# A hybrid decoder layer on eight cores: the meta tokens' projection moved into the first block, and a norm stage reordered with one operation on another engine

## Chip, cores and metric

The kernel runs on the 8 cores of one Trainium2 chip. Each core computes one batch element by itself, with the same program and the same weights, so there is no traffic between cores. The metric is the device time of the slowest core, in microseconds (us).

## The reference, cut to what matters

Per batch element: 2048 tokens of width 2048, with 16 learned meta tokens in front, and one layer.

```
u = rms_norm(h)                                   # h = [meta ; x]
z_pool | v_conv | g_conv | gate_a | gate_b = u @ w_in      # 1024|1024|1024|2048|2048 columns
y_a = causal_multiscale_pool(z_pool) @ w_pool_out          # windows 2,4,8,16
y_b = silu(layer_norm(causal_conv31(v_conv * sigmoid(g_conv)))) @ w_conv_out
m   = sigmoid(gate_a) * y_a + sigmoid(gate_b) * y_b
h   = h + rms_norm(m @ w_o)
h   = h + rms_norm(relu(rms_norm(h) @ w_up)**2 @ w_down)   # 8192 hidden
return h[:, 16:]                                  # the meta tokens are dropped
```

The meta tokens reach the output only through the causal windows: the pooling looks back 15 tokens and the convolution 30. So of the meta tokens the kernel needs only z_pool, v_conv and g_conv (3072 of the 7168 columns of `w_in`).

## The kernel before, in words

**Order of the work.** All work is added to a scheduler (`Sched`) in program order; each engine runs its own operations strictly in that order, and the scheduler puts in semaphore waits from the reads and writes of tiles. SBUF tiles lie at fixed offsets, and many of them overlap (dependencies go by 512-byte grains). DMAs of weights are issued from POOL, DMAs of x, the gain rows and the output from SP.

**Weights.** `load_w` (L291) reads 1024 rows by 512 columns of an f32 weight (2 MB in HBM) and writes it as bf16 (1 MB) into the next of the four slots of `ring`. A slot can be loaded again when its last reader on PE is done. One core makes 444 such loads, 124 of them of `w_in`.

**Meta stage (L393 to L407).** The 16 meta tokens are loaded into `xin[0]`, normalised and transposed into `uTm` (L331 to L344, L300, L305). Then for each of 6 column groups (`cg`) of `w_in`, `proj_fm` loads two ring slots and runs 64 matmuls of 16 columns (L380). The results become `halo_z` (groups 0 and 1), the first 16 columns of `c_all[j]` (groups 2 and 3, L298 and L303), and `halo_a` (groups 4 and 5: a sigmoid, L388, and a product with `c_all`, L390). In SBUF, `c_all` overlaps `xin[0]` and `xs`.

**Blocks.** The 2048 tokens are worked on in 4 blocks of 512. For block 0, `phase_A_front` (L275, `nt_front` L413 to L416) and `nt_back` (L429, L436) load x in four tiles of 128 tokens, and make the normalised, transposed `uT_all`; for the other blocks this is done inside the down projection of the block before. Then come: 6 column groups of `w_in` for z, v and g (64 matmuls of 512 columns and two loads each, pooling on DVE), with 4 gate projections and the convolution (`conv_pe`, L480: 31 matmuls per channel group with diagonal weights `dg` that DVE builds, L467) in between; four more gate projections; LayerNorm; `w_po` and `w_co`; `w_o` (L627, L637, L641).

**Norm stage (L645 to L661).** After `w_o`, for each of the four token tiles DVE and ACT compute the reciprocal norm (L313 to L322), DVE multiplies (L653) and adds the tile of x (L656), which SP loads into `xin[tt % 2]`. `xin` overlaps `csq`, into which ACT writes squares until the end of the `w_o` stage. After all four tiles, a second loop calls `nt_front` and `nt_back` for each tile: ACT squares (L413), the norm (L318 to L322), DVE scales into `xs` (L416), PE transposes 16 times 128x128 (L429), DVE multiplies by the gain into `uT_all` in two halves (L436). Then follow `w_up` (16 column groups, L380, L669, L671) and `w_down` (L627).

**PSUM.** `nb(n)` hands out the 8 banks in rotation, leaving out those in `bank_reserved`.

Of the kernel before, what the change touches and what calls it, by code (L numbers as in the profile page):

```python
# [5 lines left out]
F32 = mybir.dt.float32  # L6
BF16 = mybir.dt.bfloat16
AF = mybir.ActivationFunctionType
ALU = mybir.AluOpType
# [4 lines left out]
NMETA = 16  # L14
# [5 lines left out]
TB = 512  # L20
# [121 lines left out]
def build_program(nblk=NBLK):  # L142
# [9 lines left out]
    w_in_d = din("w_in", [D, INC])  # L152
# [18 lines left out]
    S = Sched(nc)  # L171
# [12 lines left out]
    def bump(shape, dt, name):  # L184
        nbytes = int(np.prod(shape[1:])) * (2 if dt == BF16 else 4)
        t = sb(ptr[0], shape, dt, name)
        ptr[0] += (nbytes + G - 1) // G * G
        return t
# [11 lines left out]
    halo_z = bump([128, 8, 15], F32, "haloz")  # L200
    halo_a = bump([128, 8, 30], BF16, "haloa")
    uTm = bump([128, 16, 16], BF16, "uTm")
    wgrp = bump([128, 4, 2, 256], BF16, "wgrp")
    NST = 12
    sts = [bump([128, 16], F32, f"st{i}") for i in range(NST)]
# [41 lines left out]
    def nb(n):  # L247
        r = []
        while len(r) < n:
            bk = banks[bank_rr[0] % 8]  # L250
            bank_rr[0] = (bank_rr[0] + 1) % 8
            if bk in bank_reserved:
                continue
            r.append(bk)
        return r
# [4 lines left out]
    with contextlib.ExitStack() as es:  # L260
# [24 lines left out]
        def load_w(src2d, r0, nk, c0, ncols=512):  # L285
            i = ring_rr[0]
            ring_rr[0] = (i + 1) % 4
            slot = ring[i]
            src = src2d[r0:r0 + nk * 128, c0:c0 + ncols].rearrange("(kc p) n -> p kc n", p=128)
            dst = slot.ap()[:, 0:nk, 0:ncols]  # L290
            S.add("pool", lambda e: e.dma_start(out=dst, in_=src), writes=(slot,), dma_sem=ring_sems[i])  # L291
            return slot

        def copy_scaled(dst_tile, dst_ap, src_tile, src_ap, scale_ap=None, eng=None, extra_reads=()):
            eng = eng or ev_engine()
            if eng == "act":
                if scale_ap is None:
                    f = lambda e: e.activation(out=dst_ap, in_=src_ap, func=AF.Copy)  # L298
                else:
                    f = lambda e: e.activation(out=dst_ap, in_=src_ap, func=AF.Copy, scale=scale_ap)  # L300
            else:
                if scale_ap is None:
                    f = lambda e: e.tensor_copy(out=dst_ap, in_=src_ap)  # L303
                else:
                    f = lambda e: e.tensor_scalar(out=dst_ap, in0=src_ap, scalar1=scale_ap, scalar2=None,  # L305
                                                  op0=ALU.mult)
            S.add(eng, f, reads=(src_tile,) + tuple(extra_reads), writes=(dst_tile,))
# [59 lines left out]
        S.add("dve", lambda e: e.memset(ones_f.ap(), 1.0), writes=(ones_f,))  # L367
        S.add("dve", lambda e: e.memset(halo_a.ap(), 0.0), writes=(halo_a,))

        def proj_fm(wsrc, c0, kchunks, rhs_fn, ntok, bks):  # L370
            nkh = kchunks // 8
            for kh in range(nkh):
                slot = load_w(wsrc, kh * 1024, 8, c0)
                for oc in range(4):
                    def mm(e, kh=kh, oc=oc, slot=slot):
                        inst = None
                        for k in range(8):
                            kk = kh * 8 + k
                            rt, ra = rhs_fn(kk)
                            inst = e.matmul(bks[oc].ap()[:, 0:ntok], lhsT=slot.ap()[:, k, oc * 128:(oc + 1) * 128],  # L380
                                            rhs=ra, start=(kk == 0), stop=(kk == kchunks - 1))
                        return inst
                    rd = [slot] + [rhs_fn(kh * 8 + k)[0] for k in range(8)]
                    S.add("pe", mm, reads=rd, writes=(bks[oc],))

        def glu_into(j, bank, ntok, a_tile, a_ap):
            s = sg[j % 2]
            S.add("act", lambda e: e.activation(out=s.ap()[:, 0:ntok], in_=bank.ap()[:, 0:ntok], func=AF.Sigmoid),  # L388
                  reads=(bank,), writes=(s,))
            S.add("dve", lambda e: e.tensor_tensor(out=a_ap, in0=c_all[j].ap()[:, 0:ntok], in1=s.ap()[:, 0:ntok],  # L390
                                                   op=ALU.mult), reads=(c_all[j], s), writes=(a_tile,))
# [1 line left out]
        dma_in("sp", xin[0], xin[0].ap()[0:NMETA, :], meta_d, xin_sems[0])  # L393
        norm_transpose([(xin[0], xin[0].ap()[0:NMETA, :])], NMETA, gpm,
                       lambda kc, ti: (uTm, uTm.ap()[:, kc, :]))
        for cg in range(6):
            bks = nb(4)
            proj_fm(w_in_d, cg * 512, 16, lambda kk: (uTm, uTm.ap()[:, kk, :]), NMETA, bks)
            for oc in range(4):
                j = (cg % 2) * 4 + oc  # L400
                bk = bks[oc]
                if cg < 2:
                    copy_scaled(halo_z, halo_z.ap()[:, j, :], bk, bk.ap()[:, 1:16])
                elif cg < 4:
                    copy_scaled(c_all[j], c_all[j].ap()[:, 0:NMETA], bk, bk.ap()[:, 0:NMETA])
                else:
                    glu_into(j, bk, NMETA, halo_a, halo_a.ap()[:, j, 14:30])  # L407

        def nt_front(src_t, src_ap, tt):
            xsb = xs[tt % 2]  # L410
            st = st_tile()
            ssa = st.ap()[:, 0:1]
            S.add("act", lambda e: e.activation(out=xsb.ap(), in_=src_ap, func=AF.Square, accum_out=ssa),  # L413
                  reads=(src_t,), writes=(xsb, st))
            rt, ra = rstd_from_ss(st, st.ap()[:, 0:1], 1, 1.0 / D, RMS_EPS)
            S.add("dve", lambda e: e.tensor_scalar(out=xsb.ap(), in0=src_ap, scalar1=ra, scalar2=None, op0=ALU.mult),  # L416
                  reads=(src_t, rt), writes=(xsb,))

        def nt_back(tt, gain):
            xsb = xs[tt % 2]  # L420
# [28 lines left out]
        for b in range(nblk):  # L449
# [46 lines left out]

            for cg in range(4):
                bks = nb(4)
                proj_fm(w_in_d, cg * 512, 16, u_rhs, TB, bks)
                for oc in range(4):  # L500
                    j = (cg % 2) * 4 + oc
                    bk = bks[oc]
                    if cg < 2:
                        z = zx[j % 2]
                        za = z.ap()
                        copy_scaled(z, za[:, 15:527], bk, bk.ap())
                        S.add("dve", lambda e, za=za, j=j: e.tensor_copy(out=za[:, 0:15], in_=halo_z.ap()[:, j, :]),
                              reads=(halo_z,), writes=(z,))
                        wlog = j // 2 + 1
                        src_t = z  # L510
                        for s_ in range(wlog):
                            sh = 1 << s_
                            lo = (1 << (s_ + 1)) - 1
                            dst_t = pt[s_ % 2]
                            S.add("dve", lambda e, d=dst_t.ap(), s=src_t.ap(), lo=lo, sh=sh: e.tensor_tensor(
                                out=d[:, lo:527], in0=s[:, lo:527], in1=s[:, lo - sh:527 - sh], op=ALU.add),
                                reads=(src_t,), writes=(dst_t,))
                            src_t = dst_t
                        dd = dsb[j]
                        S.add("dve", lambda e, dd=dd, s=src_t.ap(), za=za, w=float(1 << wlog): e.scalar_tensor_tensor(  # L520
                            out=dd.ap(), in0=s[:, 15:527], scalar=1.0 / w, in1=za[:, 15:527],
                            op0=ALU.mult, op1=ALU.subtract), reads=(src_t, z), writes=(dd,))
                        S.add("dve", lambda e, za=za, j=j: e.tensor_copy(out=halo_z.ap()[:, j, :], in_=za[:, 512:527]),
                              reads=(z,), writes=(halo_z,))
                    else:
                        copy_scaled(c_all[j], c_all[j].ap(), bk, bk.ap(), eng="act")
            gq = [(0, 0), (0, 1), (1, 0), (1, 1)]
            for half in range(2):
                bks = nb(4)
                proj_fm(w_in_d, (4 + half) * 512, 16, u_rhs, TB, bks)  # L530
                j0 = half * 4
                g_front(j0, bks[0])
                g_front(j0 + 1, bks[1])
                gate_proj(*gq[half * 2])
                conv_pe(j0)
                conv_pe(j0 + 1)
                g_front(j0 + 2, bks[2])
                g_front(j0 + 3, bks[3])
                gate_proj(*gq[half * 2 + 1])
                conv_pe(j0 + 2)  # L540
                conv_pe(j0 + 3)
# [106 lines left out]
            for tt in range(4):  # L648
# [6 lines left out]
                      reads=(h, rt, gbuf), writes=(h,))  # L655
                S.add("dve", lambda e, h=h, xi=xi: e.tensor_tensor(out=h.ap(), in0=h.ap(), in1=xi.ap(), op=ALU.add),  # L656
                      reads=(h, xi), writes=(h,))

            for tt in range(4):
                nt_front(hT[tt], hT[tt].ap(), tt)  # L660
                nt_back(tt, gpl)  # L661

            for cg in range(16):
# [79 lines left out]
```

How the kernel before makes its waits and increments, by code:

```python
        def run(q, e):  # L114
            waited = {}
            for op in self.queues[q]:
                need = {}
                for d in op.deps:
                    sem = d.dma_sem if d.dma_sem is not None else esems[d.eng]
                    v = d.sigval
                    if waited.get(sem, 0) < v and need.get(sem, 0) < v:
                        need[sem] = v
                for sem, v in need.items():
                    e.wait_ge(sem, v)
                    waited[sem] = v
                inst = op.fn(e)
                if op.dma_sem is not None:
                    inst.then_inc(op.dma_sem, 16)
                elif op.signals:
                    inst.then_inc(esems[q], 1)
            if q == "sp":
                for sem in final_waits:
                    e.wait_ge(sem, 16 * self.dma_cnt[sem])
```

## Time and profile before

| | us |
|---|---|
| before, median of 2 runs | 4516.17 |
| lowest and highest | 4496.57, 4535.77 |
| the profiled execution, its own time | 4061.35 |
| its span on the slowest core (core 4) | 4059.5 |
| spans of the 8 cores | 3958.0 to 4059.5 |

The profiled execution is shorter than the two timed runs by 455 us. Durations in the profile belong to that execution. Engines: PE is TensorE's matmul, PEld its weight load, DVE VectorE, ACT ScalarE, POOL GpSimd, SP SyncE. "L380" is line 380 of the kernel. A row of the timeline gives start, duration, engine, line, operation, output and input, the number of merged instructions, and in brackets how long the engine sat idle and who ended that.

### The profile page before, as it was taken

How to read it: one execution, taken by the hardware profiler on the slowest of the kernel's cores; microseconds unless marked ns; L12 is line 12 of the kernel's file. 1: busy time of each engine (PE TensorE's matmuls, PEld its weight loads, DVE VectorE, ACT ScalarE, POOL GpSimd, SP SyncE). 2: the span in 40 equal slices, each digit the busy share in tenths (PEclk: the TensorE clock that was granted, in tenths of full speed). 3: DMA queues.
4: the chain of work that ended last, by engine and by line, in shares of the span. 5: the costliest groups of instructions: out<-in, count | busy, mean ns of one | idle time of the engine just before them, and what ended most of it. 6: DMA issues, size and time to landing. Idle time of an engine off the chain costs nothing.

```text
span 4059.5 us, 40152 instructions; the slowest of 8 cores (3958.0 to 4059.5 us)
## 1 busy us (share of the span) xinstructions
PE 3418.7 (84%) x15920; PEld 1550.7 (38%) x15920; DVE 1029.8 (25%) x1350; ACT 551.7 (14%) x1010; POOL 389.3 (10%) x449
## 2 busy tenths in 40 slices
PE   1799848889999895888999985878999998488997
PEld 1344323334444342334444432333444443233443
DVE  0331541111053234112042243211104315411002
ACT  0112111110011211111001111111001121111000
POOL 1000101001110010110110010000111001011110
PEclk9999979999999997999999997899999999799998
DMA  9976979999996697999998589899999769699996
GB/s 150 160 104 88 130 134 120 117 141 136 152 181 89 93 141 132 123 129 144 151 178 123 82 127 166 92 119 123 147 153 178 112 88 130 113 119 120 137 153 125
DMA packets 472231, 527.76 MB, mean 130 GB/s; under 512 B 8928, under 2 KB 464864, under 8 KB 464864
## 3 DMA queue, kind: packets, MB, share of 16 engines
q0 software_dynamic: 462800, 466.12, 86.9%
q1 hardware_dynamic: 9248, 59.08, 4.3%
q8 instruction: 129, 2.11, 0.2%
q14 instruction: 54, 0.44, 0.0%
HBM read 974.48 MB, written 16.78 MB: 244 GB/s over the span
## 4 chain that ended last, share of the span: by engine, by line
PE 70%; DMA 22%; DVE 5%; issue 2%; ACT 1%; DVEq 0%; POOL 0%; ACTq 0%; POOLq 0%; SPq 0%
PE pb L380 35%; PE pb L627 27%; DMA ring<-w_up 15%; PE pb L480 5%; DMA ring<-w_in 4%; DMA xin<-x 3%; DVE uTall L436 1%; PE pb L564 1%; PE pb L565 1%; DVE xs L416 1%; PE pb L429 1%; DVE hT L656 1%; DVE hT L653 1%; DVE csq L587 0%; ACT xs L413 0%
## 5 line engine op out<-in xcount | busy, mean ns | idle before, releaser
L380 PE MATMUL pb<-uTall,ring 128*128 128x512 bf16 x7680 | 1730.1, 388 | 209.7 <-DMA ring<-w_up 170.0
L380 PEld LDWEIGHTS pb<-uTall,ring 128*128 128x128 bf16 x7680 | 760.6, 100 | 1177.0 <-issue 323.0
L627 PE MATMUL pb<-ring,hid 128*128 128x512 bf16 x4096 | 890.9, 381 | 9.8 <-DVE fT L637 9.8
L627 PEld LDWEIGHTS pb<-ring,hid 128*128 128x128 bf16 x4096 | 402.0, 98 | 497.4 <-issue 18.2
L671 DVE TENSOR_TENSOR hid<-rs 128x512 bf16<-128x512 f32 x256 | 177.2, 692 | 936.4 <-ACT rs L669 936.4
L669 ACT ACTIVATE rs<-pb 128x512 f32<-128x512 f32 x256 | 152.8, 597 | 979.0 <-PE pb L380 975.6
L429 PE MATMUL pb<-identb,xs 128*128 128x128 bf16 x512 | 54.3, 293 | 251.9 <-DVE xs L416 251.9
L291 POOL DMA_DIRECT2D ring<-w_up x128 | 111.9, 874 | 1190.7 <-PE pb L380 1062.8
L627 PE MATMUL pb<-ring,mT 128*128 128x512 bf16 x1024 | 221.7, 379 | 0.0
L637 DVE COPY fT<-pb 128x512 f32<-128x512 f32 x64 | 43.4, 689 | 685.7 <-PE pb L627 648.1
L480 PE MATMUL pb<-ax,dg 128*128 128x512 bf16 x992 | 217.2, 379 | 0.0
L291 POOL DMA_DIRECT2D ring<-w_in x124 | 108.4, 875 | 1109.3 <-PE pb L380 994.9
L291 POOL DMA_DIRECT2D ring<-w_dn x128 | 111.9, 874 | 868.3 <-PE pb L627 707.5
L380 PE MATMUL pb<-pB,ring 128*128 128x512 bf16 x512 | 120.7, 397 | 53.0 <-ACT pB L592 53.0
L429 PEld LDWEIGHTS pb<-identb,xs 128*128 128x128 bf16 x512 | 47.9, 135 | 259.2 <-issue 258.5
L627 PEld LDWEIGHTS pb<-ring,mT 128*128 128x128 bf16 x1024 | 100.2, 98 | 120.8
L480 PEld LDWEIGHTS pb<-ax,dg 128*128 128x128 bf16 x992 | 96.2, 97 | 118.3
L467 DVE TENSOR_TENSOR dg<-identb,wdw 128x3968 bf16<-128x3968 bf16 x32 | 137.0, 4283 | 0.0
L641 ACT ACTIVATE rs<-fT 128x512 f32<-128x512 f32 x64 | 40.1, 627 | 706.5 <-DVE fT L637 702.5
L390 DVE TENSOR_TENSOR ax<-call,sg 128x512 bf16<-128x512 f32 x32 | 22.0, 688 | 375.6 <-ACT sg L388 375.6
L380 PE MATMUL pb<-pA,ring 128*128 128x512 bf16 x512 | 113.1, 379 | 0.0
L380 PEld LDWEIGHTS pb<-pB,ring 128*128 128x128 bf16 x512 | 51.7, 102 | 120.0 <-issue 65.0
(87 smaller groups left out, 1287.4 us busy)
## 6 DMA issues: line engine op xcount, KB each, us to landing
ring<-w_up POOLq DMA_DIRECT2D x128, 1024.0 KB, 25.3
ring<-w_dn POOLq DMA_DIRECT2D x128, 1024.0 KB, 10.8
ring<-w_in POOLq DMA_DIRECT2D x124, 1024.0 KB, 11.6
xin<-x SPq DMA_DIRECT2D x32, 1024.0 KB, 9.8
ring<-w_o POOLq DMA_DIRECT2D x32, 1024.0 KB, 10.7
ring<-w_po POOLq DMA_DIRECT2D x16, 1024.0 KB, 10.8
ring<-w_co POOLq DMA_DIRECT2D x16, 1024.0 KB, 10.8
out<-fT SPq DMA_DIRECT2D x16, 1024.0 KB, 9.6
```

Of the source, the lines that this page charges most:

```text
L291: S.add("pool", lambda e: e.dma_start(out=dst, in_=src), writes=(slot,), dma_sem=ring_sems[i])
L380: inst = e.matmul(bks[oc].ap()[:, 0:ntok], lhsT=slot.ap()[:, k, oc * 128:(oc + 1) * 128], rhs=ra, start=(kk == 0), stop=(kk == kchunks - 1))
L416: S.add("dve", lambda e: e.tensor_scalar(out=xsb.ap(), in0=src_ap, scalar1=ra, scalar2=None, op0=ALU.mult), reads=(src_t, rt), writes=(xsb,))
L429: inst = e.transpose(out=bview[:, i * 128:(i + 1) * 128], in_=xsb.ap()[:, kc * 128:(kc + 1) * 128], identity=ident_b.ap())
L436: S.add("dve", lambda e, o_ap=o_ap, i0=i0, i1=i1: e.tensor_tensor(out=o_ap, in0=i0, in1=i1, op=ALU.mult), reads=(bk, gain), writes=tuple(u ...
L467: S.add("dve", lambda e, d=d, j=j: e.tensor_tensor(out=d.ap(), in0=ident_b.ap().unsqueeze(1).broadcast_to([128, KCONV, 128]), in1=wdw.ap() ...
L480: inst = e.matmul(bk.ap(), lhsT=d.ap()[:, k, :], rhs=a.ap()[:, k:k + 512], start=(k == 0), stop=(k == KCONV - 1))
L564: e.matmul(b_sum.ap(), lhsT=ones_f.ap(), rhs=c_all[j].ap(), start=(j == 0), stop=(j == 7))
L627: inst = e.matmul(bks[tt].ap(), lhsT=act_tiles[kk].ap()[:, tt * 128:(tt + 1) * 128], rhs=slot.ap()[:, k, :], start=(kk == 0), stop=(kk == ...
L637: S.add("dve", lambda e, tt=tt, og=og, bks=bks: e.tensor_copy(out=dst[tt].ap()[:, og * 512:(og + 1) * 512], in_=bks[tt].ap()), reads=(bks[ ...
L669: S.add("act", lambda e, r=r, oc=oc, bks=bks: e.activation(out=r.ap(), in_=bks[oc].ap(), func=AF.Relu), reads=(bks[oc],), writes=(r,))
L671: S.add("dve", lambda e, r=r, jj=jj: e.tensor_tensor(out=hid[jj].ap(), in0=r.ap(), in1=r.ap(), op=ALU.mult), reads=(r,), writes=(hid[jj],))
```

## The change

Two things are changed.

First, the meta stage's projection is gone as a stage of its own. The norm and the transposes of the meta tokens stay where they are. In block 0, `proj_fm` takes one more argument: with `meta_bank` it adds 64 matmuls of 16 columns (`mmeta`) behind the group's own 64, from the same two ring slots, into one more PSUM bank `mbk`. The halos are filled from `mbk`; v goes to a new tile `vm` and not to `c_all`. For the two groups of g the banks are reserved until their sigmoid.

Second, the two loops of the norm stage become one: `nt_front` and `nt_back` of a tile follow directly on its add, and the scale into `xs` is an ACT activation there and no longer a DVE operation.

```diff
+    vm = bump([128, 8, NMETA], F32, "vm")
...
-        def proj_fm(wsrc, c0, kchunks, rhs_fn, ntok, bks):
+        def proj_fm(wsrc, c0, kchunks, rhs_fn, ntok, bks, meta_bank=None):
             nkh = kchunks // 8
+            slots = []
             for kh in range(nkh):
                 slot = load_w(wsrc, kh * 1024, 8, c0)
+                slots.append(slot)
...
+            if meta_bank is not None:
+                def mmeta(e):
+                    inst = None
+                    for oc in range(4):
+                        for kk in range(kchunks):
+                            inst = e.matmul(meta_bank.ap()[:, oc * NMETA:(oc + 1) * NMETA],
+                                            lhsT=slots[kk // 8].ap()[:, kk % 8, oc * 128:(oc + 1) * 128],
+                                            rhs=uTm.ap()[:, kk, :], start=(kk == 0), stop=(kk == kchunks - 1))
+                    return inst
+                S.add("pe", mmeta, reads=slots + [uTm], writes=(meta_bank,))
...
-        for cg in range(6):
-            bks = nb(4)
-            proj_fm(w_in_d, cg * 512, 16, lambda kk: (uTm, uTm.ap()[:, kk, :]), NMETA, bks)
-            for oc in range(4):
-                j = (cg % 2) * 4 + oc
-                bk = bks[oc]
-                if cg < 2:
-                    copy_scaled(halo_z, halo_z.ap()[:, j, :], bk, bk.ap()[:, 1:16])
-                elif cg < 4:
-                    copy_scaled(c_all[j], c_all[j].ap()[:, 0:NMETA], bk, bk.ap()[:, 0:NMETA])
-                else:
-                    glu_into(j, bk, NMETA, halo_a, halo_a.ap()[:, j, 14:30])
...
             for cg in range(4):
                 bks = nb(4)
-                proj_fm(w_in_d, cg * 512, 16, u_rhs, TB, bks)
+                mbk = nb(1)[0] if b == 0 else None
+                proj_fm(w_in_d, cg * 512, 16, u_rhs, TB, bks, meta_bank=mbk)
...
+                    if b == 0:
+                        if cg < 2:
+                            copy_scaled(halo_z, halo_z.ap()[:, j, :], mbk, mbk.ap()[:, oc * NMETA + 1:(oc + 1) * NMETA])
+                        else:
+                            copy_scaled(vm, vm.ap()[:, j, :], mbk, mbk.ap()[:, oc * NMETA:(oc + 1) * NMETA])
...
+                if b == 0:
+                    for oc in range(4):
+                        j = j0 + oc
+                        sm = sg[j % 2]
+                        S.add("act", lambda e, sm=sm, oc=oc, mbk=mbk: e.activation(
+                            out=sm.ap()[:, 0:NMETA], in_=mbk.ap()[:, oc * NMETA:(oc + 1) * NMETA], func=AF.Sigmoid),
+                            reads=(mbk,), writes=(sm,))
+                        S.add("dve", lambda e, sm=sm, j=j: e.tensor_tensor(
+                            out=halo_a.ap()[:, j, 14:30], in0=vm.ap()[:, j, :], in1=sm.ap()[:, 0:NMETA], op=ALU.mult),
+                            reads=(vm, sm), writes=(halo_a,))
+                bank_reserved.update(bks)
                 g_front(j0, bks[0])
+                bank_reserved.discard(bks[0])
...
-        def nt_front(src_t, src_ap, tt):
+        def nt_front(src_t, src_ap, tt, scale_eng="dve"):
...
+            if scale_eng == "act":
+                S.add("act", lambda e: e.activation(out=xsb.ap(), in_=src_ap, func=AF.Copy, scale=ra),
+                      reads=(src_t, rt), writes=(xsb,))
...
                 S.add("dve", lambda e, h=h, xi=xi: e.tensor_tensor(out=h.ap(), in0=h.ap(), in1=xi.ap(), op=ALU.add),
                       reads=(h, xi), writes=(h,))
-
-            for tt in range(4):
-                nt_front(hT[tt], hT[tt].ap(), tt)
+                nt_front(h, h.ap(), tt, scale_eng="act")
                 nt_back(tt, gpl)
```

## Rows read from the trace of the kernel before

**Rows 1.** The profile's page: busy time by engine, and TensorE's clock by slice.

```profile
PE 3418.7 (84%) x15920; PEld 1550.7 (38%) x15920; DVE 1029.8 (25%) x1350; ACT 551.7 (14%) x1010; POOL 389.3 (10%) x449
...
PEclk9999979999999997999999997899999999799998
```

**Rows 2.** The profile's page: the chain that ended last, by line.

```profile
PE pb L380 35%; PE pb L627 27%; DMA ring<-w_up 15%; PE pb L480 5%; DMA ring<-w_in 4%; DMA xin<-x 3%; DVE uTall L436 1%; PE pb L564 1%; PE pb L565 1%; DVE xs L416 1%; PE pb L429 1%; DVE hT L656 1%; DVE hT L653 1%; DVE csq L587 0%; ACT xs L413 0%
```

**Rows 3.** Timeline of core 4, from 0 to 260 us: the meta stage and the first x tiles.

```profile
20.01 1.27 DVE L334 TENSOR_SCALAR xs<-xin,st 16x2048 bf16<-16x2048 f32 x1
...
27.59 1.86 PE L380 MATMUL pb<-uTm,ring 128*128 128x16 bf16 x64 [5.59 <-DVE uTm L305]
...
94.59 1.00 PE L380 MATMUL pb<-uTm,ring 128*128 128x16 bf16 x32 [5.86 <-DMA ring<-w_in]
...
96.73 18.52 SPq L275 DMA_DIRECT2D xin<-x  x4
106.53 1.91 ACT L413 ACTIVATE xs<-xin 128x2048 bf16<-128x2048 f32 x1 [10.29 <-DMA xin<-x]
...
122.10 1.91 ACT L413 ACTIVATE xs<-xin 128x2048 bf16<-128x2048 f32 x1 [8.92 <-DMA xin<-x]
...
125.03 1.29 DVE L416 TENSOR_SCALAR xs<-xin,st 128x2048 bf16<-128x2048 f32 x1
...
133.88 85.89 PE L380 MATMUL pb<-uTall,ring 128*128 128x512 bf16 x384 [1.39 <-DVE uTall L436]
```

**Rows 4.** What the SP queue waited for: total us, times, longest.

```profile
SPq L124 <- DVE haloa L390: 28.3, 1, 28.3
```

**Rows 5.** Ring tile, 134 to 330 us: issue to landing of the 20 loads there.

```profile
DMA to landing us min/median/max: 8.1/10.7/11.6
```

**Rows 6.** Timeline of core 4, 178 to 300 us: block 0 between gate and convolution.

```profile
234.71 13.97 PE L380 MATMUL pb<-uTall,ring 128*128 128x512 bf16 x64 [1.52 <-ACT sg L388]
```

**Rows 7.** Timeline of core 4, 520 to 605 us: the norm stage of block 0.

```profile
549.68 2.29 DVE L656 TENSOR_TENSOR hT<-hT,xin 128x2048 f32<-128x2048 f32 x1 [11.85 <-DMA xin<-x]
551.89 0.15 DVE L313 TENSOR_REDUCE st<-st 128x1 f32<-128x4 f32 x1
...
552.97 2.35 DVE L653 SCALAR_TENSOR_TENSOR hT<-hT,st,gbuf 128x2048 f32<-128x2048 f32 x1
555.49 2.29 DVE L656 TENSOR_TENSOR hT<-hT,xin 128x2048 f32<-128x2048 f32 x1 [0.17 <-DVE hT L653]
...
570.13 1.29 DVE L416 TENSOR_SCALAR xs<-hT,st 128x2048 bf16<-128x2048 f32 x1
...
571.56 1.86 PE L429 MATMUL pb<-identb,xs 128*128 128x128 bf16 x16 [39.86 <-DVE xs L416]
572.68 2.36 DVE L436 TENSOR_TENSOR uTall<-pb,gpl 128x1024 bf16<-128x1024 bf16 x2 [1.26 <-PE pb L429]
574.95 0.14 DVE L318 TENSOR_SCALAR st<-st 128x1 f32<-128x1 f32 x1
...
589.59 2.36 DVE L436 TENSOR_TENSOR uTall<-pb,gpl 128x1024 bf16<-128x1024 bf16 x2 [1.27 <-PE pb L429]
590.96 14.21 PE L380 MATMUL pb<-uTall,ring 128*128 128x512 bf16 x59 [0.63 <-DVE uTall L436]
```

**Rows 8.** Timeline of core 4, 2486 to 2556 us: the norm stage of block 2, fourth tile.

```profile
2524.45 2.29 DVE L656 TENSOR_TENSOR hT<-hT,xin 128x2048 f32<-128x2048 f32 x1 [3.49 <-DMA xin<-x]
```

**Rows 9.** Groups by line and shape, ACT: busy us, mean ns.

```profile
L413 ACT ACTIVATE xs<-hT 128x2048 bf16<-128x2048 f32 x16 | 30.4, 1897 | 0.0
...
L298 ACT ACTIVATE call<-pb 128x512 f32<-128x512 f32 x32 | 19.1, 597 | 90.4 <-PE pb L380 90.4
...
L300 ACT ACTIVATE pA<-pb,psc 128x512 bf16<-128x512 f32 x16 | 10.9, 686 | 1.9 <-PE pb L550 1.4
```

**Rows 10.** Ring tile, 592 to 875 us (up projection of block 0): issue to landing.

```profile
DMA to landing us min/median/max: 11.5/26.9/33.1
```

More of the change, by code:

```diff
@@ L415, in nt_front @@
             rt, ra = rstd_from_ss(st, st.ap()[:, 0:1], 1, 1.0 / D, RMS_EPS)
-            S.add("dve", lambda e: e.tensor_scalar(out=xsb.ap(), in0=src_ap, scalar1=ra, scalar2=None, op0=ALU.mult),
-                  reads=(src_t, rt), writes=(xsb,))
+            if scale_eng == "act":
+                S.add("act", lambda e: e.activation(out=xsb.ap(), in_=src_ap, func=AF.Copy, scale=ra),
+                      reads=(src_t, rt), writes=(xsb,))
+            else:
+                S.add("dve", lambda e: e.tensor_scalar(out=xsb.ap(), in0=src_ap, scalar1=ra, scalar2=None, op0=ALU.mult),
+                      reads=(src_t, rt), writes=(xsb,))
         def nt_back(tt, gain):
@@ L502, in build_program @@
                     bk = bks[oc]
+                    if b == 0:
+                        if cg < 2:
+                            copy_scaled(halo_z, halo_z.ap()[:, j, :], mbk, mbk.ap()[:, oc * NMETA + 1:(oc + 1) * NMETA])
+                        else:
+                            copy_scaled(vm, vm.ap()[:, j, :], mbk, mbk.ap()[:, oc * NMETA:(oc + 1) * NMETA])
                     if cg < 2:
@@ L529, in build_program @@
                 bks = nb(4)
-                proj_fm(w_in_d, (4 + half) * 512, 16, u_rhs, TB, bks)
+                mbk = nb(1)[0] if b == 0 else None
+                proj_fm(w_in_d, (4 + half) * 512, 16, u_rhs, TB, bks, meta_bank=mbk)
                 j0 = half * 4
+                if b == 0:
[9 more added lines that the diff above has]
+                bank_reserved.update(bks)
                 g_front(j0, bks[0])
+                bank_reserved.discard(bks[0])
                 g_front(j0 + 1, bks[1])
+                bank_reserved.discard(bks[1])
                 gate_proj(*gq[half * 2])
@@ L537, in build_program @@
                 g_front(j0 + 2, bks[2])
+                bank_reserved.discard(bks[2])
                 g_front(j0 + 3, bks[3])
+                bank_reserved.discard(bks[3])
                 gate_proj(*gq[half * 2 + 1])
```

## The prediction

> **What bounds the kernel now.** I read the page first. TensorE is busy 84% of the span at a clock near full, no other engine over 25% [rows 1]; the chain that ended last is TensorE for 70%, then waits for `w_up` loads (15%), `w_in` loads (4%) and x tiles (3%) [rows 2]. So the kernel is TensorE with holes in it, and the change works on two kinds of hole: the start, and the norm stage of each block. The timeline of the start shows the first: the 12 weight loads of the meta stage pass at (94.59 - 27.59) / 10 = 6.7 us each, while the 32 matmuls on each take 1.00 us. SP then sits until 96.73 before it can load x, and the first 512-column matmul runs at 133.88 [rows 3]. What it waited for last is the halo's product on DVE, which reads `c_all`, on top of which x is to be loaded [rows 4]. The timeline of the norm stage shows the second: from the first add of x at 549.68 to the first `w_up` matmul at 590.96, 41.28 us, DVE and ACT work through four tiles and TensorE does only transposes [rows 7].
>
> **Part 1, the start.** Twelve loads and 384 small matmuls leave the start, 384 come back in block 0. `vm` takes the place of `c_all`, so the load of x into `xin[0]` waits only for the meta norm, whose last read ends at 20.01 + 1.27 = 21.3 [rows 3]; SP's issue is at about 21.4 in place of 96.73. From that issue to the first block matmul it was 133.88 - 96.73 = 37.15, which contains the landing of two x tiles beside four weight loads still under way, the wait for the next two, and the norms. In the new kernel three to four weight loads are under way at 21.4, so I take the same 37.15: first matmul at 58.6, a gain of 75.3 us. Bounds: if x were to land only behind three weight loads (3 x 6.7 = 20 us, in place of beside them), everything is some 19 us later and the gain is 56; if x lands with less company than before, the 10.3 and 8.9 us that ACT waited for it [rows 3] could lose a third, and the gain is 82.
>
> **Part 2, the meta matmuls in block 0.** They are now on TensorE's own path, behind each of six groups. 64 of them take 1.86 us in one run and 2.00 in two runs of 32 [rows 3]: 6 x 2.0 = +12.0. Block 0 has TensorE working 13.97 us per 64 matmuls, 6.98 per load [rows 6], and loads land 8.1 to 11.6 us after issue [rows 5], so nothing but TensorE sets the pace there and nothing hides the 12 us. Low bound 0 (if the loads set the pace instead), high bound the spacing of the transposes, 1.86 / 16 = 0.116 us each [rows 7], 45 us.
> The Trainium skill's page "TensorE: Matmul & The Clock Gate", section "LDWEIGHTS (loading the stationary operand)", puts a weight load at its columns divided by 1.2 per ns, 107 ns for 128 columns whatever follows; a 16-column matmul can't cover that. By it the 384 pairs would cost 41 us, 29 more than my term. The trace disagrees: 64 pairs passed in 1.86 us, 29 ns each.
>
> Two edges of this part. The two slots of a group are now both held until the meta matmuls behind it, so POOL, whose next load waits for the slot's last reader, issues in pairs every 15.97 us and no longer one per 6.98. Behind it in POOL's queue stand only further weight loads. The first of a pair is needed 15.97 us later, the second 22.9 us later; with a landing of at most 11.6, and one more load's 6.7 for the second (18.3), both are in time, at no cost. And the rotation of the banks shifts in block 0: the gate projection behind the first convolutions no longer needs a bank that waits for a sigmoid, which gives back its 1.52 us [rows 6]: -1.5, with 0 and -3 as bounds. Four small sigmoids and products stand before the first g half's work on DVE; DVE then has the 14 us of a gate projection as cover for two `dg` builds, as before. On SP the four x loads pass nothing else of weight.
>
> **Part 3, the norm stage.** DVE runs strictly in program order. Before, its adds for all four tiles stood ahead of the norms, and ACT's work on one tile ran beside DVE's on the next. Now DVE carries for each tile: norm, multiply, add, then it waits for ACT's square, computes the norm, waits for ACT's scale, for PE's transposes, and does the two gain products; only then comes the next tile's multiply. Queued behind these waits are all later DVE operations of the stage, and TensorE waits for the last of them. The period of a tile, from the reduce to the next reduce: reduce to multiply 552.97 - 551.89 = 1.08; multiply to add 2.52; the add 2.29 [rows 7]; hand-over 0.15; square to the scale's start 125.03 - 122.10 = 2.93 [rows 3]; the scale on ACT 1.90 + 0.09 = 1.99 (the 2048-wide activation, plus what a scale operand added to the 512-wide one, 686 - 597 ns) [rows 9]; hand-over 0.14; transposes to first product 572.68 - 571.56 = 1.12; both products 574.95 - 572.68 = 2.27 [rows 7]. Sum 14.49.
> From the first add to the first `w_up` matmul: 4 x 14.49, less the first tile's 1.08 and 2.52 (they lie ahead of that add), less the last pair's 2.27 and plus 590.96 - 589.59 = 1.37 (the matmuls start after the first of the two): 53.5 against 41.3, +12.2 us. In block 2 the fourth tile's add waited 3.49 for x [rows 8]; that wait is hidden now, so +8.5 there. Four blocks: 3 x 12.2 + 8.5 = +45.1. The scale's move alone is 0.70 of the period. Bounds: if the tiles overlapped in spite of the order, the stage would be DVE's work alone, about 37 us, -17 in all; if hand-overs are each worse, +60. Does anything hide it? All four ring slots are full in the stage, so no loading is gained, and TensorE's clock is at its lower level (1.2 GHz) there before and after.
>
> **Sum.** -75.3 + 12.0 - 1.5 + 45.1 = -19.7 us. The gain at the start is nearly all given back. The profiled execution is 4061.35, so 4041.7, a factor of 0.9951. The timed runs lie 455 us above it, which no row explains; I carry the factor over: 4516.17 x 0.9951 = 4494.
>
> **The rivals.**
> 1. The loads set the pace. The loads of `w_in` passed at 6.7 us and TensorE takes 6.98 per load: a margin of 4%. The timed runs are 455 us longer; if all that sat in the 444 loads it would be 1.02 us each, and block 0 would be bound by loads. Then the 12 loads taken away are worth 12 us more and the meta matmuls cost nothing: -44, 4472. Against it: the landings of 8 to 12 us in block 0 [rows 5].
> 2. The norm stage overlaps after all (ACT takes work off DVE, a tile's norm runs beside the next one's add): -17 in place of +45.1, -81.7 in all, factor 0.980, 4425. For it: DVE is the busiest in the stage; against it: DVE's strict order, in which every term above is a chain.
> 3. Slower: the held slots starve TensorE in block 0. If the first load of a pair took the 26.9 us that `w_up` loads take from issue to landing under pressure [rows 10], and not 10.7, each group would wait 26.9 - 15.97 = 10.9, six groups 66: +46 in all, factor 1.0113, 4567. It decides as soon as the wait is over 19.7 / 6 = 3.3 us a group. Against it: [rows 5].
> 4. Each meta matmul carries its whole weight load (PEld's own time per load, were it not overlapped): the price is inside the bounds of part 2, up to +45 in place of +12.0, so +13 in all, 4531. Against it: the 29 ns of [rows 3].
>
> **How the numbers follow.** My forecast 0.60; the loads set the pace 0.20; overlap 0.05; starved groups 0.12; full weight loads 0.03. The range has to hold 8 in 10: the forecast, rival 1 and rival 4 with the spread of the two runs shown (20 us each way) and the bounds of the start (56 to 82) reach from about 4440 to 4550; overlap and the worst of the starved case stay out: 4435 to 4550. A measurement of this kernel can tell about 2% from no change, that is 4426 and 4606. Faster by over 2%: half of the overlap and a small part of rival 1, and what I have not thought of: 0.08. Slower by over 2%: the starved case beyond its price, 0.05. Within 2%: 0.87.
>
> **What would show it.** In the new timeline: x issued by SP near 21 us and the first 512-column matmul near 59; behind each of the first six groups 64 matmuls of 16 columns in about 2 us; POOL's loads of block 0 in pairs, with no wait of TensorE for `w_in` worth naming there; in the norm stage, four adds of x some 14.5 us apart (5.8 before), DVE idle for ACT's scale, and 53 us from the first add to the first `w_up` matmul. I am wrong if the adds stand under 10 us apart, if the first block matmul comes after 70, if TensorE waits over 3 us for a load in each group of block 0, or if the up projection, which no part of the change touches, comes out longer or shorter by tens of us.

## The result, and the profile after

| | us |
|---|---|
| changed kernel, median of 39 runs | 4063.98 |
| kernel before, median of 37 runs | 4132.47 |
| ratio | 0.992, 95% interval 0.9898 to 0.9943 |
| the changed kernel's profiled execution, its time and span | 4035.21, 4033.7 |

Both medians include executions in which the cores of one die show a lower granted clock than the other's (one of the kernel before: 4490.94 us, about 0.80 on one die and 0.94 on the other); the ratio, here and below, compares only the undisturbed ones.

So the change makes the kernel 0.8% faster, some 32 us in 4060 (23 to 41), which is inside the 2% that the prediction called "no change". The time itself, 4063.98, lies far below the stated range of 4435 to 4550.

The start, in the timeline of the changed kernel's slowest core (core 5), answers to [rows 3]:

```profile
24.31 19.24 SPq L276 DMA_DIRECT2D xin<-x  x4
...
34.85 1.91 ACT L413 ACTIVATE xs<-xin 128x2048 bf16<-128x2048 f32 x1 [7.13 <-DMA xin<-x]
...
61.52 15.72 PE L383 MATMUL pb<-uTall,ring 128*128 128x512 bf16 x64 [1.42 <-DVE uTall L440]
...
94.12 13.97 PE L383 MATMUL pb<-uTall,ring 128*128 128x512 bf16 x64
...
94.81 1.75 POOL L292 DMA_DIRECT2D ring<-w_in  x2 [13.67 <-PE pb L393]
...
107.93 1.76 PE L393 MATMUL pb<-uTm,ring 128*128 128x16 bf16 x64
...
109.55 13.97 PE L383 MATMUL pb<-uTall,ring 128*128 128x512 bf16 x64
110.24 1.75 POOL L292 DMA_DIRECT2D ring<-w_in  x2 [13.69 <-PE pb L393]
```

SP issues x at 24.3 and the first 512-column matmul comes at 61.5. Two groups start 109.55 - 94.12 = 15.43 us apart, with the 64 meta matmuls between them, and POOL issues its loads in pairs. What TensorE waited for from 61 to 465 us (total us, times, longest), and the landing of the loads from 61 to 160 us (for [rows 5]):

```profile
PE pb L383 <- ACT pB L618: 13.2, 1, 13.2
PE pb L383 <- DVE uTall L440: 1.4, 1, 1.4
PE pb L590 <- ACT csq L586: 1.1, 1, 1.1
```

```profile
DMA to landing us min/median/max: 9.3/15.3/16.2
```

No load is waited for in block 0, and the sigmoid's wait of [rows 6] is gone. The norm stage of block 0, same core, answers to [rows 7]:

```profile
481.20 2.29 DVE L682 TENSOR_TENSOR hT<-hT,xin 128x2048 f32<-128x2048 f32 x1 [10.93 <-DMA xin<-x]
483.58 1.91 ACT L413 ACTIVATE xs<-hT 128x2048 bf16<-128x2048 f32 x1 [16.12 <-DVE hT L682]
...
486.56 2.00 ACT L417 ACTIVATE xs<-hT,st 128x2048 bf16<-128x2048 f32 x1 [0.41 <-DVE st L323]
488.81 1.87 PE L433 MATMUL pb<-identb,xs 128*128 128x128 bf16 x16 [24.67 <-ACT xs L417]
489.93 2.36 DVE L440 TENSOR_TENSOR uTall<-pb,gpl 128x1024 bf16<-128x1024 bf16 x2 [3.52 <-PE pb L433]
492.20 0.14 DVE L314 TENSOR_REDUCE st<-st 128x1 f32<-128x4 f32 x1
...
495.81 2.29 DVE L682 TENSOR_TENSOR hT<-hT,xin 128x2048 f32<-128x2048 f32 x1 [0.17 <-DVE hT L679]
...
535.20 10.10 PE L383 MATMUL pb<-uTall,ring 128*128 128x512 bf16 x44 [0.62 <-DVE uTall L440]
```

The adds stand 14.61 us apart (5.81 before), and the chain from one to the next is the one that the prediction wrote out: add, square, scale, transposes, products, and only then the next tile's norm. DVE sits idle for 3.52 us before the products.

Each core's trace was cut by the starts of instructions into stages: start (to the first 512-column matmul), block 0's matmuls up to the last of `w_o`, the same of blocks 1 to 3, the four waits from there to the first add of x, the four norm stages (first add to first `w_up` matmul), the four up projections (to the first `w_down` matmul), the four down projections. Means over the eight cores, in us; for the up projections also the least and the most of a core:

```
kernel             start  block0  1 to 3  to add  norm   up (a core's sum)    down
before             135.6  396.6   1216.2   63.5   170.1  1074 (1016 to 1111)  967
changed             60.4  402.7   1218.2   66.9   216.9  1082 (1062 to 1097)  968
e1 fold only        58.8  403.0   1215.3   63.4   168.3  1057 (1042 to 1071)  967
e2 norm only       133.3  397.0   1215.8   65.1   217.0  1061 (1031 to 1076)  968
e3 meta twice       59.1  412.6   1214.0   61.6   216.9  1029 (1014 to 1042)  968
e4 pipelined, ACT   59.0  402.7   1229.1   67.0   122.4  1048 (1025 to 1067)  967
e5 one loop, DVE    59.2  402.6   1228.9   61.5   203.6  1043 ( 994 to 1066)  971
e6 two loops, ACT   59.4  402.3   1221.5   60.4   182.9  1041 (1014 to 1066)  973
e7 pipelined, DVE   59.4  402.9   1215.1   68.1   116.6  1061 (1047 to 1071)  974
e8 up from w_in     59.3  402.9   1215.9   36.1   216.8   889 ( 888 to  890)  964
e9 other pitch      59.0  422.5   1221.4   34.2   216.9   898 ( 889 to  917)  976
e10 tiled w_up      59.2  402.4   1215.1   65.8   112.6   891 ( 888 to  892)  965
```

(In e4 to e6 one pair of cores or another lost some 28 us within a block to a lower clock; that is in "1 to 3". In e9 four cores lost time in this way, two of them some 80 us in block 0.) Two things are to be seen here. The touched stages moved as forecast: start -75.2, block 0 +6.1, norm stages +46.8, together -22.3 (the forecast's terms: -75.3, +10.5, +45.1). And the up projections, which the change does not touch, differ by up to 54 us in their means from one profiled execution to the next, with the same `w_up` loads, and by up to 95 from core to core within one: more than the change is worth.

### The profile page after: what moved, and what is told of

Its sections match the earlier page's. It is cut to its first block, busy times and chain, and to the rows that moved or that the text cites. A ratio compares the mean times of both kernels' runs of the same rounds, so it can differ in the third digit from the quotient of the medians.

```text
span 4033.7 us, 40131 instructions; the slowest of 8 cores (3991.3 to 4033.7 us)
## 1 busy us (share of the span) xinstructions
PE 3407.6 (84%) x15920; PEld 1547.4 (38%) x15920; DVE 1012.7 (25%) x1334; ACT 579.9 (14%) x1024; POOL 378.8 (9%) x437
## 4 chain that ended last, share of the span: by engine, by line
PE 70%; DMA 20%; DVE 5%; ACT 3%; issue 2%; SPq 0%; DVEq 0%; ACTq 0%; POOLq 0%
PE pb L383 36%; PE pb L653 26%; DMA ring<-w_up 14%; PE pb L484 5%; DMA ring<-w_in 2%; DMA xin<-x 2%; ACT xs L413 1%; DMA ring<-w_dn 1%; DVE uTall L440 1%; DVE hT L682 1%; ACT xs L417 1%; PE pb L590 1%; DVE hT L679 1%; PE pb L591 1%; PE pb L433 1%
## 5 line engine op out<-in xcount | busy, mean ns | idle before, releaser
L292 POOL DMA_DIRECT2D ring<-w_in x112 | 97.9, 875 | 1058.1 <-PE pb L383 787.9
```

## The experiments

**e1, the first part alone.** The changed kernel with the norm stage in its old form:

```diff
-                nt_front(h, h.ap(), tt, scale_eng="act")
-                nt_back(tt, gpl)
+
+            for tt in range(4):
+                nt_front(hT[tt], hT[tt].ap(), tt)
+                nt_back(tt, gpl)
```

> Only the first part of the change: the meta projection is folded into block 0, the norm stage is as before. My theory (the terms are right and stand side by side): the first block matmul at about 60 us in place of 135, block 0 from there to the last w_o matmul some 6 to 9 us longer, the rest unchanged: 66 to 70 us off, ratio 0.983. Rival (loads set the pace and the gain at the start is partly met again later, or multiplied): a ratio under 0.978 or over 0.988.

Measured: ratio 0.9809 (0.9778 to 0.984), some 77 us; start 58.8, block 0 +6.4, the rest as before. The ratio lies between the rival's two bounds; its interval just touches the lower one, 0.978.

**e2, the second part alone.** The kernel before, with `nt_front` of the changed one and

```diff
-
-            for tt in range(4):
-                nt_front(hT[tt], hT[tt].ap(), tt)
-                nt_back(tt, gpl)
+                nt_front(h, h.ap(), tt, scale_eng="act")
+                nt_back(tt, gpl)
```

> Only the second part of the change: one loop in the norm stage with the scale on ACT, meta stage as before. My theory (DVE's strict order makes a chain of it): first add to first w_up matmul 54 us in place of 41 to 45, so +46 us in all, ratio 1.011. Rival (the changed kernel is 32 us faster where the steps of the trace add up to some 22, because this part costs less than it seems, for instance since the up projection behind it gives some back): a ratio of 1.005 or less.

Measured: ratio 1.0105 (1.0075 to 1.0135), +42 us; norm stages 217.0 in place of 170.1. So the second part, by itself, makes the kernel slower; the rival's 1.005 lies outside the interval. The product of both ratios is 0.9912 against 0.992 for both together: the parts stand side by side.

**e3, the meta matmuls twice.**

```diff
                 S.add("pe", mmeta, reads=slots + [uTm], writes=(meta_bank,))
+                S.add("pe", mmeta, reads=slots + [uTm], writes=(meta_bank,))
```

> The changed kernel with every group's 64 meta matmuls issued twice (the result is the same). If their price is what the changed kernel's trace shows between the groups (15.43 - 13.97 = 1.46 us each), block 0 gets 6 x 1.5 = 9 us longer from the first block matmul to the last w_o matmul. If loads set the pace there, it gets no longer. If a meta matmul carried a whole weight load, the second set would add over 30 us.

Measured: block 0 412.6 against 402.7, +9.9 us for 384 more matmuls, 26 ns each. They are on TensorE's path, no load hides them, and none adds the time of a whole weight load to it (a weight load's own record lasts 95 ns). (This execution was all the same shorter than the changed kernel's profiled one, because of its up projections, 1029 against 1082: a single execution says nothing of a few tens of us here.)

**e4, the norm stage interleaved.** After `w_o` the four multiplies come first; then, in this order (each a few lines with the operations of before):

```diff
-                nt_front(h, h.ap(), tt, scale_eng="act")
-                nt_back(tt, gpl)
...
+            add_x(0)
+            square(0)
+            add_x(1)
+            norm_scale(0)
+            square(1)
+            nt_back(0, gpl)
+            norm_scale(1)
+            add_x(2)
+            square(2)
+            nt_back(1, gpl)
+            norm_scale(2)
+            add_x(3)
+            square(3)
+            nt_back(2, gpl)
+            norm_scale(3)
+            nt_back(3, gpl)
```

> The changed kernel with the norm stage written in another order: all four multiplies first (beside the wait for x), then adds and norms interleaved so that DVE always has a tile's add or product to do while ACT squares or scales another; the scale stays on ACT. If it is the order of DVE's queue that costs the 54 us and not the engine of the scale, first add to first w_up matmul falls to 28 to 32 us, under the 41 to 45 of the kernel before: 4 x 24 = 96 us off the changed kernel, ratio to before about 0.970. If ACT is what bounds the stage (16 us of squares and scales) or x lands too late, 35 to 40 us and a ratio of about 0.98.

Measured: 122.4 / 4 = 30.6 us a stage, ratio 0.9737 (0.9689 to 0.9786). Same operations, same engines as in the changed kernel, another order: 23.6 us less a stage. Its timeline (core 1, block 0) shows the third and the fourth add 6.6 us apart, with ACT's scale beside them (the first two stand 2.2 us apart, the second and third 9.4):

```profile
492.01 2.29 DVE L690 TENSOR_TENSOR hT<-hT,xin 128x2048 f32<-128x2048 f32 x1
492.22 2.00 ACT L705 ACTIVATE xs<-hT,st 128x2048 bf16<-128x2048 f32 x1 [0.42 <-DVE st L323]
...
495.66 2.36 DVE L440 TENSOR_TENSOR uTall<-pb,gpl 128x1024 bf16<-128x1024 bf16 x2 [1.36 <-PE pb L433]
...
498.58 2.29 DVE L690 TENSOR_TENSOR hT<-hT,xin 128x2048 f32<-128x2048 f32 x1
...
510.17 20.05 PE L383 MATMUL pb<-uTall,ring 128*128 128x512 bf16 x86 [0.69 <-DVE uTall L440]
```

**e5 and e6, order and engine apart.** e5 is the changed kernel with `scale_eng="dve"` in its one loop; e6 has two loops as in e1, but with `scale_eng="act"`.

> The changed kernel with one loop in the norm stage, but the scale back on DVE. By my sum the engine of the scale is 0.70 us and a hand-over of 0.3 out of a tile's 14.6: first add to first w_up matmul 50 to 52 us in place of 54. If the move to ACT were the dear part, it would fall back to 41 to 45.

> The changed kernel with the norm stage in two loops as before, but the scale on ACT. If the order is what costs, first add to first w_up matmul is 44 to 46 us (the 41.3 of before, plus 4 tiles of about 1 us). If the engine is what costs, it stays at 52 to 54.

Measured on core 5, block 0; e5, then e6, timelines:

```profile
478.08 2.29 DVE L682 TENSOR_TENSOR hT<-hT,xin 128x2048 f32<-128x2048 f32 x1 [9.62 <-DMA xin<-x]
...
528.70 16.59 PE L383 MATMUL pb<-uTall,ring 128*128 128x512 bf16 x70 [0.62 <-DVE uTall L440]
```

```profile
479.35 2.29 DVE L682 TENSOR_TENSOR hT<-hT,xin 128x2048 f32<-128x2048 f32 x1 [10.91 <-DMA xin<-x]
...
496.78 2.29 DVE L682 TENSOR_TENSOR hT<-hT,xin 128x2048 f32<-128x2048 f32 x1 [0.17 <-DVE hT L679]
...
524.30 10.91 PE L383 MATMUL pb<-uTall,ring 128*128 128x512 bf16 x43 [0.69 <-DVE uTall L440]
```

One loop with DVE's scale 50.6, two loops with ACT's 45.0, against 41.3 (neither) and 54.0 (both). So in block 0 the order costs 9.0 to 9.3 us a stage and the engine 3.4 to 3.7; they add. Over all cores and blocks the table gives 8.4 to 8.5 and 3.2 to 3.3.

**e7, interleaved, scale on DVE.** e4 with the scale as a DVE operation.

> The interleaved norm stage with the scale on DVE. There DVE has a tile's add or product waiting for it, so its 1.29 us is added to its own queue but the 0.7 us shorter scale and one hand-over less shorten each tile's chain: 28 to 32 us from first add to first w_up matmul, within 2 us of the form with ACT, ratio to before 0.970 to 0.976. If the move to ACT pays once DVE is the busier engine, 2 us or more longer per block than the form with ACT (29.8 to 31).

Measured: 116.6 / 4 = 29.2 us a stage (30.6 with ACT), ratio 0.9692 (0.9633 to 0.9752). Even where DVE is busy, ACT's longer scale and its hand-over do not pay in the traces; the ratios of the two can't be told apart.

**e8, the up projection with w_in's weights.** What remained was the scatter of the up projections. A load reads 2 KB pieces, one of each row; from a piece to the next (the pitch) it is 32 KB in `w_up`, whose rows have 8192 numbers of 4 bytes, and 28 KB in `w_in`. Left out: the up projection's true weights.

```diff
-                proj_fm(w_up_d, cg * 512, 16, u_rhs, TB, bks)
+                proj_fm(w_in_d, (cg % 14) * 512, 16, u_rhs, TB, bks)
```

> The changed kernel, in which the up projection reads its weights from w_in (row pitch 28 KB, the 16 column groups taken modulo 14) in place of w_up (row pitch 32 KB): the same count and size of loads and the same matmuls, on other numbers. It asks what makes the up projection last 240 to 285 us, and what makes this time scatter from run to run by more than the change is worth. If the loads of w_up are slow because of where they lie, the stage falls to 220 to 230 us on all cores, with little scatter, and 160 us or more come off. If the stage is slow because 8 cores load at once whatever they load, it stays at 260 or more.

Measured: every core 222 us a stage, sums of 888 to 890; the cores' spans are 3780 to 3786 where the changed kernel's were 3991 to 4034. The loads of one such stage (core 2, 510 to 750 us), against [rows 10]:

```profile
DMA to landing us min/median/max: 9.0/9.9/17.6
```

The wait ahead of the first add fell too, from 66.9 to 36.1 in four. SP issues x at 464 us, while the first four loads of the coming up projection, issued from 444 to 465 us, are under way (core 5, block 0): beside loads of `w_up` the x tiles took a median of 16.7 us to land, beside loads of `w_in` 9.3.

**e9, the same buffer at another pitch.** Left out, again: the true weights.

```diff
+    w_up_v = w_up_d.rearrange("a (b c) -> (a b) c", b=4)
...
-                proj_fm(w_up_d, cg * 512, 16, u_rhs, TB, bks)
+                proj_fm(w_up_v[(cg // 4) * 2048:(cg // 4 + 1) * 2048, :], (cg % 4) * 512, 16, u_rhs, TB, bks)
```

> The changed kernel, in which the up projection reads the same buffer w_up as if it were a matrix of 8192 rows of 2048 (pitch 8 KB in place of 32 KB): same buffer, same number, size and piece length (2 KB) of reads, other numbers. If the pitch of 32 KB is what makes w_up's loads slow and the up projection scatter, the stage falls to about 222 us on every core as it did with w_in's 28 KB. If it is the place of the buffer or its size, it stays at 250 to 280.

Measured: on the four cores that kept their clock throughout, 889 to 891 for the four stages and spans of 3780 to 3782; of the 32 stages of all cores 28 took 222 to 223 us. The loads of one stage on core 5:

```profile
DMA to landing us min/median/max: 9.3/10.0/10.5
```

It is not the buffer and not its size: 2 KB pieces with a pitch of 32 KB are slow here, pieces of the same length with 8 or 28 KB are not. (No run read another buffer at 32 KB.)

**e10, both findings in one correct kernel.** e7, and `w_up` stored by the host as 16 column groups one behind the other:

```diff
-    w_up_d = din("w_up", [D, DFF])
+    w_up_d = din("w_up", [16 * D, 512])
...
-                proj_fm(w_up_d, cg * 512, 16, u_rhs, TB, bks)
+                proj_fm(w_up_d[cg * D:(cg + 1) * D, :], 0, 16, u_rhs, TB, bks)
...
-        "w_up": f(np.asarray(w_up)[0]),
+        "w_up": f(np.asarray(w_up)[0].reshape(D, 16, 512).transpose(1, 0, 2).reshape(16 * D, 512)),
```

> All of the computation, correct: the interleaved norm stage with the scale on DVE, and w_up handed to the kernel in another layout (the host stores its 16 column groups of 512 one after the other, so that a load reads 2 MB in one piece; no arithmetic, and not timed). If the two gains add up: up projection 4 x 222, norm stage 4 x 29, x loads 8 us sooner at each norm stage, so 3785 (the span with w_in's weights) less 4 x 25 = about 3685, ratio to before 0.905 to 0.92. If reading in one piece is slower than 2 KB pieces with a pitch, or the down projection takes the scatter over, 3750 or more.

Measured: 3717.97 and 3713.93 us in its two undisturbed runs of six, where the kernel before took 4008 to 4031 on the same chip: about 0.924, too few runs for an interval. That misses the 3685 and the 0.905 to 0.92 expected. Two lines of its page, and two of its cores:

```profile
PE 3349.4 (90%) x15612; PEld 1543.0 (42%) x15920; DVE 1030.6 (28%) x1350; ACT 547.2 (15%) x1008; POOL 378.8 (10%) x437
...
PE pb L383 48%; PE pb L653 29%; PE pb L484 6%; DMA ring<-w_in 2%; DMA xin<-x 1%; DVE uTall L440 1%; PE pb L433 1%; PE pb L590 1%; PE pb L591 1%; DMA ring<-w_dn 1%; DVE xs L705 1%; DVE csq L613 1%; DVE hT L690 0%; ACT xs L413 0%; DVE hT L680 0%
```

```profile
core 0: 3716.4 us, clock 0.957
...
core 3: 3708.1 us, clock 0.957
```

`w_up` has left the chain of waits [rows 2]. The 30 us over the forecast stand in the wait to the first add: 65.8, not 36, which is 16.5 us in each block on every core. In the interleaved form the four multiplies stand ahead of the first add in DVE's queue, and here DVE goes from the last of them to the adds without a wait for x (core 0, block 0):

```profile
476.13 2.35 DVE L680 SCALAR_TENSOR_TENSOR hT<-hT,st,gbuf 128x2048 f32<-128x2048 f32 x1
478.40 4.49 DVE L690 TENSOR_TENSOR hT<-hT,xin 128x2048 f32<-128x2048 f32 x2
```

The late x used to hide them. Moving that add behind the first multiply was not tried.

## Why the prediction was right or wrong

**The step that failed is the last one of the sum: the base.** "The timed runs lie 455 us above it, which no row explains; I carry the factor over" took 4516, from two runs, as the measure of this kernel. In the later runs of the kernel before, times of that size (4423 to 4491 us) come only with one die at a granted clock near 0.80, and the undisturbed ones take 4008 to 4066; the clocks of the two runs themselves are not on record, so that they were of this kind is read from their times. The factor was 0.9951; measured is 0.992 (0.9898 to 0.9943), so it is a little outside the interval. Applied to the profiled execution's own 4061.35 it gives 4042, within 0.6% of the measured median; the undisturbed runs of the changed kernel lie at 3983 to 4036. The forecast of a change within 2%, with the gain at the start nearly given back, holds; by size, 20 us were forecast and 23 to 41 measured. With two runs 11% above a profiled execution, that execution's time should have been inside the range.

**Part 1, the start: right.** -75.3 forecast, -75.2 as a mean over the cores. On core 5 the issue came at 24.3 and not at 21.4, because the constants landed later (DVE's first operation at 18.03, 15.36 before); from there it was 61.5 - 24.3 = 37.2, as taken. The last tenths of the agreement are luck: the forecast was made from core 4 (133.9), the mean before was 135.6, and so the mean hides the 2.9; core 4 itself went from 133.9 to 61.5, -72.4.

**Part 2, the meta matmuls: right in kind, too dear.** The term was 6 x 2.0 = 12.0. In a stream with the large ones before and behind them they take 15.43 - 64 x 0.2158 = 1.62 us a group (0.2158 is 13.81 / 64, the gate projections' spacing in the chain of waits), 9.7 in all, and e3 gives 9.9. The 2.0 was read from durations, which hold the end of the last matmul too, and not from starts. The bank's 1.5 came back as forecast. A further gain of some 1.3 was not thought of: the first large matmuls stand 427 ns apart and the later ones 216, some 14 of them before and 8 after (the profile gives the granted clock as 1.00 in both stretches, so it does not say why). That makes 9.7 - 1.5 - 1.3 = +6.9; the mean over the cores is +6.1, the forecast was +10.5.
On the rule of the Trainium skill's page "TensorE: Matmul & The Clock Gate", section "LDWEIGHTS (loading the stationary operand)", e3 settles it: 107 ns a weight load, one behind the other, would by estimate be 41 us, and 26 ns a pair were measured, so the loads overlap; the rule gives the time of one load, and that nothing could cover it was the prediction's reading. The same page's section "Wait — 56ns, not 53.3ns?" gives a floor of about 25 ns from start to start, however few columns; this agrees.

**The held slots: right.** Loads come in pairs 15.43 us apart and land after 9.3 to 16.2 us (at most 11.6 before, one at a time); TensorE waits for none. Rival 3 fell. For the second of a pair the forecast had at most 18.3.

**Part 3, the norm stage: right.** The granted clock in the stage is 0.50 before and after, as taken. Period 14.49 forecast, 14.61 measured; stage 53.5 against 54.0; four stages +45.1 against +46.8. ACT's scale was 2.00 (1.99 forecast). That the order is the greater part of the cost is shown by e5 and e6, though the engine costs more than "0.70 of the period" per tile says: 3.4 to 3.7 a stage is 0.9 a tile, the hand-over included. Rival 2, overlap, came only in another order (e4), which shows what it needed. Its price was set too high, "DVE's work alone, about 37 us": that counts work ahead of the first add. DVE is busy for 27.1 us of the changed kernel's stage, and the interleaved stages took 30.6 and 29.2.

**Rival 1, loads set the pace: fell** for block 0 (e3: the extra matmuls cost their full time). It was built on the same 455 us as the base.

**What stays open.** The touched stages give -22.3 us in the profiled executions, the timed runs -23 to -41, middle -32. If there is a rest, some 10 us, it most likely lies in the up projections, since all else is steady to a few us, but this is not shown. Whether the change shifts them a little (the kernel before had a mean of 1074, the other variants with the same loads 1029 to 1061, but the changed kernel itself 1082) can't be told from single executions, and it wasn't tried further. The prediction's sign of error, an up projection longer or shorter by tens of us, did not show in the mean (+8), and with this scatter it could not have told much.

## What to carry to other kernels

Two loops joined into one, on an engine whose queue is in program order, were slower here because the joined body waits for other engines: every wait is then exposed once per tile. Keep the independent work of the next tile between the question and the answer, as e4 does, and only then ask which engine should do the scale. A stage that scatters by more than the change is worth, in traces of kernels that all leave it alone, is itself the thing to look at; here it held some 225 us (193 in the up projections, 31 in the waits ahead of the first adds, by e8), seven times the gain. And a timed median from two runs is no base until it is laid beside the profiled execution's own time.

## What the runs showed of the hardware

Reads of 2 KB pieces whose rows lie 32 KB apart, by eight cores at once, land after a median of 26.9 us and pull the up projection out to 240 to 287 us, scattered [rows 10]; with 28 KB (e8) or 8 KB in the same buffer (e9) they land after about 10 us and the stage takes 222 on every core that keeps its clock. That the pitch was the cause is shown for these three pitches and these buffers; what in the memory makes it so isn't, and no run had fewer than eight cores. The Trainium skill's page "DMA: Bandwidth & Descriptors", section "Why small descriptors are slow (HBM only)", looks at the size of a piece; here the size is the same in the slow and the quick case.
